# The last tile before three norms worked out in two halves of 256 tokens, and the three tiles behind each norm as well

## What is computed

```python
def first_block(x, c, norm1_g, norm2_g, ada_w, ada_b, w_in, w_fourier, w_ret, w_out,
              ffn_up, conv_w, conv_b, ffn_down, final_g):
    c_act = jax.nn.silu(c)
    for l in range(DEPTH):                      # DEPTH = 2
        mod = (c_act @ ada_w[l] + ada_b[l])[:, None, :]
        sh1, sc1, g1, sh2, sc2, g2 = jnp.split(mod, N_MOD, axis=-1)
        h = rmsnorm(x, norm1_g[l]) * (1.0 + sc1) + sh1
        x = x + g1 * token_mix(h, w_in[l], w_fourier[l], w_ret[l], w_out[l])
        h = rmsnorm(x, norm2_g[l]) * (1.0 + sc2) + sh2
        x = x + g2 * conv_ffn(h, ffn_up[l], conv_w[l], conv_b[l], ffn_down[l])
    return rmsnorm(x, final_g)
```

## Time and profile before

| | |
|---|---|
| median of 3 runs | 2971.75 us (2971.58 to 2974.42) |
| the profiled execution, its own time | 2975.31 us |
| its span in the trace | 2973.5 us |
| TensorE busy | 2940.7 us, 99% of the span |
| VectorE, ScalarE, GpSimd busy | 1787.5, 1126.8, 235.7 us |

### The profile page before, as it was taken

The page is one execution under the profiler, slowest core; times in us unless marked ns, Lnnn a source line. Parts: engine busy times, 40 slices in busy tenths (PEclk is TensorE's granted clock), DMA queues, the critical chain, the costliest instruction groups (busy, mean ns, idle before and its releaser), DMA issues. The chain is left out here.

```text
span 2973.5 us, 36519 instructions
## 1 busy us (share of the span) xinstructions
PE 2940.7 (99%) x14873; PEld 2501.1 (84%) x14873; DVE 1787.5 (60%) x2624; ACT 1126.8 (38%) x1704; POOL 235.7 (8%) x198
## 2 busy tenths in 40 slices
PE   7999999999999999999999999999999999999999
PEld 6888888888888888888888889888889887888887
DVE  7767666764867677667856646322347668543233
ACT  4433332433434333323433435222235457432222
POOL 0300000000001200200000011000002006200000
PEclk9999999999999999999999999999999999999999
DMA  7454356344443433344444435222235341222322
GB/s 289 154 184 143 127 181 193 131 139 141 142 135 107 156 126 111 119 140 134 149 138 138 137 118 181 96 100 99 92 113 171 108 149 36 71 80 98 99 94 70
DMA packets 110056, 385.83 MB, mean 130 GB/s; under 512 B 12216, under 2 KB 15672, under 8 KB 109888
## 3 DMA queue, kind: packets, MB, share of 16 engines
q1 hardware_dynamic: 84960, 296.36, 29.8%
q10 hardware_dynamic: 24928, 87.12, 9.0%
HBM read 381.32 MB, written 2.11 MB: 129 GB/s over the span
## 5 line engine op out<-in xcount | busy, mean ns | idle before, releaser
L2291 DVE TENSOR_TENSOR WL<-stage,WH 128x1024 fp32r<-128x1024 f32 x505 | 626.6, 1242 | 557.7 <-ACT WH L1528 557.5
L509 PE MATMUL ps<-HH,WH 128*128 128x512 f32 (+1 forms) x2184 | 851.8, 390 | 0.9 <-DVE WL L2291 0.9
L510 PE MATMUL ps<-HL,WH 128*128 128x512 f32 (+1 forms) x2184 | 848.5, 389 | 0.0
L511 PE MATMUL ps<-HH,WL 128*128 128x512 f32 (+1 forms) x2184 | 848.1, 388 | 0.0
L1528 ACT ACTIVATE WH<-stage 128x1024 fp32r<-128x1024 f32 x509 | 534.6, 1053 | 441.4 <-PE ps L511 428.7
L509 PE MATMUL ps<-GH,WH 128*128 128x512 f32 (+2 forms) x1660 | 572.6, 345 | 3.2 <-DVE WL L2281 2.4
L510 PE MATMUL ps<-GL,WH 128*128 128x512 f32 (+2 forms) x1660 | 571.0, 344 | 0.0
L511 PE MATMUL ps<-GH,WL 128*128 128x512 f32 (+2 forms) x1660 | 571.0, 344 | 0.0
L511 PEld LDWEIGHTS ps<-HH,WL 128*128 128x128 f32 x2184 | 410.0, 188 | 85.6
L509 PEld LDWEIGHTS ps<-HH,WH 128*128 128x128 f32 x2184 | 410.2, 188 | 83.7 <-issue 1.6
L510 PEld LDWEIGHTS ps<-HL,WH 128*128 128x128 f32 x2184 | 410.3, 188 | 81.5
(11 more groups left out here) (301 smaller groups left out, 2941.6 us busy)
## 6 DMA issues: line engine op xcount, KB each, us to landing
stage<-ws SPq DMA_DIRECT2D x535, 512.0 KB, 3.3
MST<-wm ACTq DMA_DIRECT2D x154, 512.0 KB, 3.3
Z<-wm SPq DMA_DIRECT2D x10, 512.0 KB, 8.0
TAB<-consts ACTq DMA_DIRECT2D x7, 448.0 KB, 3.7
MST<-wm SPq DMA_DIRECT2D x6, 512.0 KB, 7.4
Z<-max_rows ACTq DMA_DIRECT2D x8, 256.0 KB, 4.2
out<-X SPq DMA_DIRECT2D x16, 128.0 KB, 1.8
X<-xT SPq DMA_DIRECT2D x4, 256.0 KB, 5.5
```

The source lines that it names most:

```text
L509: e.matmul(o, wh, mh, start=start, stop=False, **more)
L510: e.matmul(o, wh, ml, start=False, stop=False, **more)
L511: return e.matmul(o, wl, mh, start=False, stop=stop, **more)
L2291: e.tensor_tensor(wl, src, wh.bitcast(F32), ALU.subtract).then_inc(wlo.sem, wlo.up(("w", i)))
```

## The change

The last tile ahead of each of the three norms is made in two halves of 256 tokens: all its blocks for tokens 0 to 255 (24 or 33 matmuls of 256 columns), then the same weights for tokens 256 to 511. The statistics of the first half are taken between matmuls of the second. Behind the norm three tiles are made together (before two), for tokens 0 to 255 and then 256 to 511, with the statistics of the second half between the matmuls of the first. The `warm` matmuls at these norms are gone. The three chunks of these tiles are split into rows 12 to 17 of GH and GL, not into WH and WL; `ahead` becomes 3 and 4 for tiles 5 and 6, and 4 and then 5 within `halved`. SP's list is as it was.

On TensorE:

```diff
+            def last_of_stage(k, name, nk, spec, ready):
+                outs = [take_bank((*name, s), dv, "x", *name, s) for s in range(2)]
+                held_blocks = []
+                for s, p in enumerate(outs):
+                    for j in range(nk):
+                        if s == 0:
+                            pe.wait_ge(lo, *ready(j))
+                            held_blocks.append((*block(spec(j)), cur["n"]))
+                        wh, wl, chunk = held_blocks[j]
+                        mh, ml = slot(j)
+                        inst = mm3(p[:, 0:256], wh, wl, mh[:, half(s)], ml[:, half(s)], j == 0, j == nk - 1)
...
+                        if s and nk == 8:
+                            if j == 1:
+                                first_norm_sums(k, 0)
+                                last_norm_sums(k, 0)
+                            elif j == 5:
+                                norm_spread(k, 0)
+                            elif j == 7:
+                                first_norm_sums(k, 1)
+                        elif s:
+                            if j == 2:
+                                first_norm_sums(k, 0)
+                                last_norm_sums(k, 0)
+                            elif j == 6:
+                                norm_spread(k, 0)
```

On ACT and DVE (each a list of its own, written out; the start of those for 8 blocks):

```diff
+            def halved(k, name, bias, free, nk):                       # ACT
...
+                    weights(name, ahead=4)
+                    square_half(0)
+                    high_half(0, 0)
+                    high_half(1, 0)
+                    square_half(1)
+                    high_half(2, 0)
+                    weights(name, ahead=5)
+                    high_half(3, 0)
...
+            def halved(k, name, gate, mod, gain, bias, nk):            # DVE
...
+                    weights(name, ahead=4)
+                    x_half(0)
+                    rms_half(0)
+                    affine_half(0, 0)
+                    affine_half(1, 0)
+                    x_half(1)
+                    low_half(0, 0)
...
-                    weights(("o", l, n))
+                    if n < 7:
+                        weights(("o", l, n), ahead=AHEAD if n < 5 else n - 2)
```

More of the change, by code:

```diff
@@ L380, in early_up @@
         def early_up(i):
-            a = upto.get("early_up")
-            return i - a if a is not None and 0 <= i - a < 3 else None
+            for k in EARLY_GROUPS:
+                a = upto.get(("early", k))
+                if a is not None and 0 <= i - a < 3:
+                    return i - a
+            return None
+        EARLY_GROUPS = [("n2", 0), ("n1", 1), ("n2", 1), ("an", 2, 0)]
         def operands(i):
@@ L394, in operands_free @@
             if early_up(i) is not None:
-                return mm, "sum", NH - 1, 5, 1
+                g = [k for k in EARLY_GROUPS if ("early", k) in upto and 0 <= i - upto["early", k] < 3][0]
+                if g == ("an", 2, 0):
+                    return mm, "sum", NH - 1, 5, 1
+                if g == ("n1", 1):
+                    return mm, "w", upto["early", ("n2", 0)] + 2
+                return mm, "yr", g[1], 7
             i -= NW
@@ L635, in rms_last, with first_norm_sums @@
                 stat["free"] = (freed_by, freed)
+            def first_norm_sums(k, s):
+                if s:
+                    p = take_bank(("hb", k), dv, "aff", k, 7, 1)
+                else:
+                    stat_free()
+                    p = STAT
+                pe.wait_ge(*added_by(k, 6))
+                for t in (2 * s, 2 * s + 1):
+                    e.matmul(p[:, t:t + 1], SSQ[:, t * 128:t * 128 + 128], OC[:, 0:1], start=t == 2 * s, stop=False,
+                             skip_group_check=True)
@@ new lines, in last_norm_sums, with norm_spread @@
+            def last_norm_sums(k, s):
+                p = norm_stat(k, s)
+                pe.wait_ge(sq, "sq", k, 7, s)
+                for t in (2 * s, 2 * s + 1):
+                    inst = e.matmul(p[:, t:t + 1], SA("sq", k, 7)[:, t * 128:t * 128 + 128], OC[:, 0:1], start=False, stop=True,
+                                    skip_group_check=True)
+                done(inst, ("ss", k, s), *([("ss", k)] if s else []))
+            def norm_spread(k, s):
+                p = norm_stat(k, s)
+                pe.wait_ge(power, k, s)
+                for t in (2 * s, 2 * s + 1):
+                    inst = e.matmul(p[:, t * 128:t * 128 + 128], V4[:, 4 + t:5 + t].to_broadcast([128, 128]), IDN[:, :],
+                                    start=True, stop=True)
+                done(inst, ("bc", k, s), *([("bc", k)] if s else []))
+                if s == 0:
+                    stat["free"] = (dv, ("aff", k, 7, 0))
@@ new lines, in halves @@
+            def halves(k, names, spec, outs, nk):
+                close()
+                upto[("early", k)] = cur["n"] + 1
+                parts = []
+                for s in range(2):
+                    for t in range(8):
+                        if s == 0:
+                            parts.append([(*block(spec(i, t)), cur["n"], cur["used"] == 8) for i in range(len(names))])
+                        mh, ml = (x[:, half(s)] for x in hx(t))
+                        pe.wait_ge(hi, "h", k, t, s)
+                        for (wh, wl, _, _), p in zip(parts[t], outs):
+                            e.matmul(p[:, half(s)], wh, mh, start=t == 0, stop=False)
+                            e.matmul(p[:, half(s)], wl, mh, start=False, stop=False)
+                        if s == 0 and nk == 8:
+                            if t == 2:
+                                norm_spread(k, 1)
+                        elif s == 0:
+                            if t == 1:
+                                last_norm_sums(k, 1)
+                        pe.wait_ge(lo, "h", k, t, s)
+                        for name, (wh, _, chunk, full), p in zip(names, parts[t], outs):
+                            inst = e.matmul(p[:, half(s)], wh, ml, start=False, stop=t == 7)
+                            if s and t == 7:
+                                done(inst, name, ("w", chunk))
+                            elif s and full:
+                                done(inst, ("w", chunk))
+                        if s == 0 and nk == 8:
+                            if t == 0:
+                                last_norm_sums(k, 1)
+                        elif s == 0:
+                            if t == 0:
+                                first_norm_sums(k, 1)
+                            elif t == 2:
+                                norm_spread(k, 1)
+                close()
+                walk.tick()
@@ L1576, in token_mix @@
                     weights(ahead=AHEAD)
[L1577 to L1582, removed]
+                    k = ("n1", l)
+                    for t in range(DT):
+                        affine_one(k, t, S, hx, lambda t: MOD[:, l, t:t + 1])
+                        weights((k, t), ahead=1)
                 if l == 0:
@@ L2397, in token_mix @@
                 k = ("n1", l)
[L2398 to L2407, removed]
+                if l == 0:
                     for t in range(1, 7):
```

251 lines of the change are left out of this document (216 added, 35 removed).

## The result

The changed kernel takes 2981.06 us (median of 8 runs, 2980.17 to 2981.76), the kernel before 2973.50 beside it (median of 8, 2971.58 to 2974.60): a ratio of 1.0024 with an interval of 1.0015 to 1.0034. It is slower by 7.6 us. The profiled execution took 2981.76, 1.8 more than its span; the profiled execution of before took 2975.31, 6.45 less. That one lies 1.81 above the median of its kernel, this one 0.70 above its own, so the 7.56 of the medians and the 6.45 of the two traces are the same difference. In a few executions TensorE's clock is lower throughout and the time much longer; the ratios leave them out.

The account below looks back on a forecast made before the run. TensorE, busy 2940.7 of 2973.5 us, was taken as the bound. -22.9 + 3.7 + 8.4 + 6.2 + 5.2 + 3.1 = +3.7 us, 2975.4 on the median, stated as 2975.0; range 2967.5 to 2981.0.

Parts of the forecast that it names:

- border of 5.9 us: About 0.2% of the time: what a measurement of this kernel tells from no change.
- Halves: 297 matmuls of 512 columns split into two of 256, each pair costing 0.0125 us more than a whole: +3.7 us.
- Sums and spreads: TensorE's statistics sums and spreads, placed between matmuls at the three norms, still cost time: +8.4 us.
- The first half is late: TensorE waits 1.9, 1.5 and 2.3 us for the first half's square at the norms, plus 0.5 behind: +6.2 us.
- The chunk that has not come: Third norm: ACT's split awaits a chunk loaded behind context loads, so TensorE waits for ACT's high part: +5.2 us.
- Clock: TensorE's clock falls to half: 1.7 us after the chunk wait, one fall of 1.4 at the norms: +3.1 us.
- The slower rival: Third norm: the chunk lands 9.8 us after issue, TensorE waits 10.1, the clock falls twice: +10.3, 2982 us; chance 0.18.
- Its base: The kernel before's median, 2971.75 us, on which the sum of +3.7 gives 2975.4.
- Its signs: Expected trace: square waits at each norm; at the third, some 5 us wait for HH, then a clock of 0.5.
- The sign that would have spoken against it: TensorE waiting for WL in the next stage, where DVE has little slack, would make the prediction wrong.
- -22.9: TensorE's time between products at the three norms, 22.9 us (0.77%), the most the change could remove.
- 10.8: Gain in us if nothing waited: 22.9 less 3.7 for halves and 8.4 for sums and spreads.

Follow-up runs that it names:

- fourth edit: The second edit, and DVE also adds epsilon to the first sums ahead of the chunk split: 2966.63 us, ratio 0.9976 to the kernel before.
- last edit: The fourth edit, and at the second norm alone DVE's split waits for POOL's power: 2965.64 us, ratio 0.9973 to the kernel before.
- first edit: The changed kernel with one more weight chunk loaded ahead of the context loads: 2973.02 us, ratio 1.000 to the kernel before.
- second: The first edit, with the first half of X (DVE) and its square (ACT) ahead of the fourth-chunk split at all three norms: 2968.95 us, ratio 0.9985.
- third (second run): The first edit plus four warm matmuls between the first two and last two first-half sums at the three norms, run again: 2970.25 us, ratio 0.9988.

## Why the prediction was right and wrong

The forecast was 2975.0, with a sum of +3.7 and a range of 2967.5 to 2981.0; measured was 2981.06, +7.6. So the time lies at the very top of the range. By the prediction's own border of 5.9 us the kernel is slower, to which it gave 0.24, and not the same, to which it gave 0.64. The mechanisms are those that it named; one term was much too small.

- *Halves, +3.7.* Right. The 30 matmuls of 256 columns from 516.58 to 520.17 take 0.1197 each, which gives 3.8.
- *Sums and spreads, +8.4.* Right. At the first norm of the fourth edit, from the first sums to the spread, 522.79 - 520.14 less 0.17 of wait and twelve matmuls (1.44) leaves 1.04 for the four sums, and the spread costs 0.44; forecast were 0.96 and 0.43. Six times that is 8.9.
- *The first half is late, +6.2.* Right in mechanism, too large: 1.50, 1.11 and 1.72 were measured, and 0.20 before the first product of the third norm, 4.5 in all. X of tile 6 at the first norm was forecast for 517.78 and started at 517.66; the half itself for 521.33, and started at 521.19. The experiments bear out the cause, the split in front of the half.
- *The chunk that has not come, +5.2.* 5.51, at the place forecast, but partly by luck. The landing took 3.8 and not the 4.9 of the earlier trace rows, and the issue of the context loads took 5.01 and not 3.65; the two errors nearly cancel. The working also has a slip: 1399.2 + 1.0 + 0.5 is 1400.7 and not 1400.5.
- *Clock, +3.1.* **The term that was mis-sized**: "I count one fall at 1.4". There were three at the norms, 1.4 each by the experiments, and the one behind the chunk lasted nearly 7 us and cost 3.0 instead of 1.7: 7.2, so 4.1 more than forecast. (The 3.0 is the difference of two stretches. The 27 matmuls from 1401.16 to 1407.03 alone take 5.87 us instead of 3.24 at full clock, 2.6.) The price of a fall was right and their number was not. The prediction allowed 0 to 3 of them and took one; the changed kernel had one at each norm, in the execution that was traced.
- *The slower rival* put a loss over 0.2% down to a landing of 9.8 us. That did not happen. The loss came to that size through the clock, which the rival had only as an addition.
- *Its base.* The sum was laid on 2971.75, a median of three. The kernel before measured 2973.50 in eight runs beside the changed one, which is 1.8 of the 6.1 us between forecast and result.
- *Its signs.* The wait of some 5 us and the clock of 0.5 behind it came as told. The sign that would have spoken against it, a wait for WL in the stages behind the norms, is in none of the three.

With the measured terms: -22.9 + 3.8 + 8.9 + 4.5 + 5.5 + 7.2 = +7.0, against +6.8 of the stretches.

The gain of the change was there all the time; two orders of instructions, and the falls of the clock that came with their waits, ate it. With both orders mended the same idea is worth 7.4 us in the median. The stretches of the last edit sum up to 80.91 against 90.88 of before, 10.0 less; the prediction had 10.8 for a change in which nothing waits.

## What to carry to other kernels

When a load's consumer is moved earlier in an in-order list, look for the load in the issuing queue and for what stands in front of it there. Here the loss went when the load was moved ahead as well, and also when the consumer was put back to the end of its list. Work that is put ahead of a step on the critical chain (here a weight split ahead of a half tile, then ahead of epsilon) delays that step: the split of 1.22 us cost TensorE 1.1 to 1.7 us in the one place and 0.8 to 0.9 in the other. It belongs where the chain leaves that engine a gap.

Count a fall of the clock, 1.2 to 1.5 us, at each place where TensorE waits long beside one-column matmuls, and not at one of them. In the traces of the changed kernel, of the first edit and of the one with ACT's split last, TensorE waits 1.1 to 1.7 us for the square at nine places, and the clock fell at eight. In the second, third (second run), fourth and last edit no single wait at these twelve places is over 0.91, and it fell at none. The 1.2 is from the first norm with ACT's split last, 28.88 with a fall against 27.66 of the first edit without one.

## What the hardware showed beyond what was expected

The length of a wait doesn't fix whether the clock falls. At the first norm TensorE waited 1.50 us in the changed kernel and 1.51 in the first edit; it ran at 1.2 GHz behind it in the one and at 2.4 in the other. In the kernel before it fell at the second and third norm, where the waits are 0.36 and less, and not at the first, where one is 0.93. And the clock was still granted in full while TensorE stood still from 1396 to 1400 (1.00), in the middle of the wait of 5.51, and was at 1.2 GHz when the work came back.

POOL's operation on 128x2 elements takes 1.76 us instead of 0.70 when it starts 0.02 us behind a DVE split with two inputs in SBUF. In the last edit, with the split held until the power was done, it took 0.70 in the same place. The Trainium skill (SBUF — State Buffer, "Who interferes with whom") says that a DVE instruction with two inputs in SBUF contends with a GpSimd instruction that reads SBUF, that the shared port pair is an exclusive lock, and that the order of issue decides who blocks. The trace agrees for POOL behind DVE. For DVE behind POOL it shows no block: the split at 521.74, 0.05 behind POOL's start, took its usual 1.23.
